# The first two blocks of a streaming encoder step: squares by quarters, early weight splitting, and one block's rstd taken from rows through DRAM

## The reference

```python
def rms_norm(x, g):
    x32 = x.astype(jnp.float32)
    y = x32 * lax.rsqrt(jnp.mean(x32 * x32, axis=-1, keepdims=True) + RMS_EPS)
    return (y * g.astype(jnp.float32)).astype(x.dtype)

def mixer_layer(x, hist_a, hist_b, norm_g, w_in, ...):
    hn = rms_norm(x, norm_g)
    proj = jnp.einsum('btd,de->bte', hn, w_in)          # 1024 -> 3584
    h_a, b_a, c_a, z_a, a_b, g_b, z_b = jnp.split(proj, SPLITS, axis=-1)
    conv_a, new_a = causal_dwconv(hist_a, c_a * h_a, conv_a_w)
    out_a = b_a * conv_a * jax.nn.silu(z_a)
    conv_b, new_b = causal_dwconv(hist_b, a_b * jax.nn.sigmoid(g_b), conv_b_w)
    s_b = jax.nn.silu(layer_norm(conv_b + conv_b_bias, ln_b_g, ln_b_b))
    out_b = s_b * jax.nn.silu(z_b)
    return x + jnp.concatenate([out_a, out_b], -1) @ w_out, new_a, new_b
```

## Time and profile before

| | |
|---|---|
| median of 3 runs | 1561.45 us (1558.83 to 1563.66) |
| the profiled execution | 1561.79 us, of which its span is 1560.0 us |
| TensorE busy | 1535.2 us, 98% of the span |
| VectorE, GpSimd, ScalarE busy | 81%, 37%, 34% |
| granted TensorE clock over the span | 0.999 |
| DMA, mean over the span | 230 GB/s, 358 MB |

### The profile page before, as it was taken

One profiled execution on the slowest core, in us unless ns is written; L12 is line 12 of the kernel. 1 busy time (PEld: TensorE's weight loads), 2 busy tenths in 40 slices (PEclk: granted clock), 3 DMA queues, 4 the chain that ended last, 5 costly groups with the idle time before them and its releaser, 6 DMA issues. The chain is left out here.

```text
span 1560.0 us, 19222 instructions
## 1 busy us (share of the span) xinstructions
PE 1535.2 (98%) x7228; PEld 1353.4 (87%) x7228; DVE 1265.7 (81%) x1179; ACT 538.1 (34%) x782; POOL 577.2 (37%) x494
## 2 busy tenths in 40 slices
PE   6999999999999999999999999999999999999998
PEld 6999999988888888888888888888897888888886
DVE  7699799998877998869798888789897577778753
ACT  5443433332242333332253312234524332332322
POOL 2766969112313121132221141146955233322310
PEclk9999999999999999999999999999999999999999
DMA  4987979788987789988779877757645433544432
GB/s 162 341 317 271 338 272 320 257 277 288 291 276 243 230 250 296 294 290 245 232 236 291 256 237 249 216 173 220 203 119 194 162 104 139 180 170 171 159 127 83
DMA packets 109648, 358.03 MB, mean 230 GB/s; under 512 B 16676, under 2 KB 20644, under 8 KB 105976
## 3 DMA queue, kind: packets, MB, share of 16 engines
q1 hardware_dynamic: 109560, 356.86, 69.6%
HBM read 263.02 MB, written 93.79 MB: 229 GB/s over the span
## 5 line engine op out<-in xcount | busy, mean ns | idle before, releaser
L1723 DVE SCALAR_TENSOR_TENSOR ps<-v,conv_b_taps,ps 128x920 f32<-128x920 f32 (+2 forms) x580 | 630.9, 1088 | 17.8
L1955 PE MATMUL ps<-xf,w_ring 128*128 128x460 f32 (+1 forms) x1624 | 603.0, 371 | 1.4 <-issue 0.9
L1957 PE MATMUL ps<-xf,w_ring 128*128 128x460 f32 (+1 forms) x1624 | 602.6, 371 | 0.0
L1956 PE MATMUL ps<-xf,w_ring 128*128 128x460 f32 (+1 forms) x1624 | 600.8, 370 | 0.0
L1955 PEld LDWEIGHTS ps<-xf,w_ring 128*128 128x128 f32 x1624 | 305.4, 188 | 36.1 <-issue 3.0
L1956 PEld LDWEIGHTS ps<-xf,w_ring 128*128 128x128 f32 x1624 | 305.4, 188 | 34.0
L1957 PEld LDWEIGHTS ps<-xf,w_ring 128*128 128x128 f32 x1624 | 304.9, 188 | 34.2
L1279 ACT ACTIVATE sets<-ps 128x460 f32<-128x460 f32 x168 | 92.8, 553 | 488.6 <-PE ps L1957 488.4
L1085 POOL TENSOR_TENSOR sets<-sets 128x460 f32<-128x460 f32 x42 | 56.1, 1335 | 415.4 <-ACT sets L1279 415.4
L1955 PE MATMUL ps<-w_out_split,mixed 128*128 128x512 f32 x512 | 199.9, 390 | 1.8 <-POOL mixed L1110 1.1
L1956 PE MATMUL ps<-w_out_split,mixed 128*128 128x512 f32 x512 | 199.5, 390 | 0.0
(11 more groups left out here) (173 smaller groups left out, 1665.1 us busy)
## 6 DMA issues: line engine op xcount, KB each, us to landing
w_ring<-weight_forms SPq DMA_DIRECT2D x294, 512.0 KB, 5.3
x_rows_again<-in_x_prompt SPq DMA_DIRECT2D x32, 512.0 KB, 4.3
out_y_prompt<-h_rows SPq DMA_DIRECT2D x32, 512.0 KB, 3.0
weight_forms<-xf SPq DMA_DIRECT2D x7, 2048.0 KB, 13.3
weight_forms<-w_ring SPq DMA_DIRECT2D x7, 2048.0 KB, 14.7
w_ring_f<-in_w_in SPq DMA_DIRECT2D x56, 256.0 KB, 3.2
xf_f<-in_w_in SPq DMA_DIRECT2D x26, 512.0 KB, 8.9
x_row<-in_x_prompt SPq DMA_DIRECT2D x28, 460.0 KB
```

Source lines behind the costliest of these rows:

```text
L1723: dve.scalar_tensor_tensor(dst, window, wb[:, j, k:k + 1], part, ALU.mult, ALU.add).then_inc(taps_done, 1)
L1955: pe.matmul(out, ahi, bhi, start=(start and x == 0), stop=False, skip_group_check=goes_on)
L1956: pe.matmul(out, ahi, blo, start=False, stop=False, skip_group_check=goes_on)
L1957: mm = pe.matmul(out, alo, bhi, start=False, stop=(stop and x == len(terms) - 1), skip_group_check=goes_on)
```

## The change

Four things are changed, all at the start of the program.

1. Block 0 comes in four quarters of 460 KB. ScalarE squares a quarter at a time, and VectorE adds each to a running sum as it comes.
2. The splitting of the first weights moves ahead: ScalarE does `weight_high(0, ...)` before the mean square of block 0, and VectorE does `weights_low(0)` as a whole before it scales x.
3. Block 1's mean squares no longer come from the channel-major copy. Its rows are loaded by four more transfers (`first_rows`, 115 partitions of 4096 bytes each, into ring space that the weights of period 1 use later), and ScalarE squares and sums each (`first_row_square`). These transfers stand between `load_w(0)` and `load_w(1)`; the channel-major block 1 now comes after `load_w(1)`.
4. Block 1's rstd is written to DRAM and read back into `spread`, behind the seven small loads on SP, and VectorE scales block 1 from there. `first_statistics(1)` and `first_rstd(1)` are gone from TensorE, and eight identity products are left of ten.

```diff
@@ -279,12 +279,10 @@
-        first_squares = [xf_f32[:, 6, :, :],
-                         ring_f32[:, 4:8, :, :].rearrange("p c l m -> p (c l m)")[:, 0:2 * HALF * TB]
-                         .rearrange("p (k t) -> p k t", t=TB)]
-
-        def first_stats(b):
-            return ps[0:STAT_ROWS, FIRST_BANK[b], 0:STAT_COLS]
+        first_squares = xf_f32[:, 6, :, :]
+        first_rows = ring_f32[0:STAT_ROWS, 4:8, :, :].rearrange("p c l m -> p c (l m)")
+        first_stats = ps[0:STAT_ROWS, FIRST_BANK, 0:STAT_COLS]
@@ -659,6 +661,8 @@
                 sp.wait_ge(rstd_out, 16 * stat_count(w, b))
+                if stat_count(w, b) == 1:
+                    sp.wait_ge(x01_scaled, 2 * KC)
                 need(sp, x_scaled, 8 * (stat_count(w, b) - 1))
@@ -818,17 +822,27 @@
+            for r in range(4):
+                src = A["xT"][0, :, r // 2].rearrange("p (k t) -> p k t", t=TB)
+                k = slice(2 * (r % 2), 2 * (r % 2) + 2)
+                sp.dma_start(st[:, r // 2, k, :], src[:, k]).then_inc(first_x_in[r], 16)
+            sp.dma_start(gain[:, :], A["norm_g"]).then_inc(gain_in, 16)
+            load_w(0)
+            for c in range(STAT_COLS):
+                sp.dma_start(first_rows[:, c, :], prompt_rows(1)[:, c, :]).then_inc(first_rows_in[c], 16)
+            load_w(1)
             for x in range(2):
-                src = A["xT"][0, :, x].rearrange("p (k t) -> p k t", t=TB)
-                sp.dma_start(st[:, x, :, :], src).then_inc(first_x_in[x], 16)
-            sp.dma_start(gain[:, :], A["norm_g"]).then_inc(gain_in, 16)
-            for x in range(2, 4):
-                src = A["xT"][1, :, x % 2].rearrange("p (k t) -> p k t", t=TB)
-                sp.dma_start(st[:, x, :, :], src).then_inc(first_x_in[x], 16)
-            load_w(0)
-            load_w(1)
+                src = A["xT"][1, :, x].rearrange("p (k t) -> p k t", t=TB)
+                sp.dma_start(st[:, 2 + x, :, :], src).then_inc(first_x_in[4 + x], 16)
             for dst, src in consts:
                 sp.dma_start(dst, src).then_inc(const_in, 16)
+            sp.wait_ge(x_rstd, 2)
+            at = P * STAT_COLS
+            dst = rstd_d[0, at:at + TB].rearrange("(r c) -> r c", c=STAT_COLS)
+            sp.dma_start(dst, x_rs[0:STAT_ROWS, STAT_COLS:2 * STAT_COLS]).then_inc(first_rstd_out, 16)
+            sp.wait_ge(first_rstd_out, 16)
+            sp.dma_start(spread[:, 0:TB], rstd_d[:, at:at + TB].to_broadcast([P, TB])).then_inc(first_rstd_in, 16)
             load_w(2)
@@ -963,6 +977,8 @@
                 pool.wait_ge(x_ms, count)
+                if count == 4:
+                    pool.wait_ge(first_rstd_out, 16)
                 need(pool, rstd_out, 16 * (count - 4))
@@ -1121,6 +1137,9 @@
             x_row_rstd(0, 1)
+            pool.wait_ge(first_row_sq, STAT_COLS)
+            pool.tensor_tensor(x_var[0:STAT_ROWS, STAT_COLS:2 * STAT_COLS], x_sq_sum[0:STAT_ROWS, STAT_COLS:2 * STAT_COLS],
+                               eps[0:STAT_ROWS, :].to_broadcast([STAT_ROWS, STAT_COLS]), ALU.add).then_inc(x_ms, 1)
             x_row_rstd(1, 2)
@@ -1188,15 +1207,20 @@
         def _(act):
-            def first_square(b, h):
-                act.wait_ge(first_x_in[2 * b + h], 16)
-                act.activation(first_squares[b][:, HALF * h:HALF * (h + 1), :], st[:, 2 * b + h, :, :], ACT.Square,
-                               scale=RMS_SCALE).then_inc(first_sq, 1)
-
-            def first_mean_square(b):
-                act.wait_ge(first_stat, b + 1)
-                act.activation(x_var[0:STAT_ROWS, STAT_COLS * b:STAT_COLS * (b + 1)], first_stats(b), ACT.Identity,
+            def first_square(r):
+                act.wait_ge(first_x_in[r], 16)
+                act.activation(first_squares[:, 2 * r:2 * r + 2, :], st[:, r // 2, 2 * (r % 2):2 * (r % 2) + 2, :],
+                               ACT.Square, scale=RMS_SCALE).then_inc(first_sq, 1)
+            def first_mean_square():
+                act.wait_ge(first_stat, 1)
+                act.activation(x_var[0:STAT_ROWS, 0:STAT_COLS], first_stats, ACT.Identity,
                                bias=eps[0:STAT_ROWS, :]).then_inc(x_ms, 1)
+            def first_row_square(c):
+                act.wait_ge(first_rows_in[c], 16)
+                act.activation(first_rows[:, c, :], first_rows[:, c, :], ACT.Square, scale=RMS_SCALE,
+                               accum_out=x_sq_sum[0:STAT_ROWS, STAT_COLS + c:STAT_COLS + c + 1]).then_inc(first_row_sq, 1)
@@ -1346,21 +1370,22 @@
-            first_square(0, 0)
-            first_square(0, 1)
-            first_square(1, 0)
-            first_square(1, 1)
-            act.wait_ge(ready0, 7)
-            first_mean_square(0)
+            for r in range(4):
+                first_square(r)
             weight_high(0, 0)
             weight_high(0, 1)
+            act.wait_ge(ready0, 7)
+            first_mean_square()
+            first_row_square(0)
+            first_row_square(1)
+            first_row_square(2)
             first_x_high(0, 0)
-            first_mean_square(1)
             first_x_high(0, 1)
+            first_row_square(3)
+            first_x_high(0, 2)
+            first_x_high(0, 3)
             weight_high(1, 0)
             weight_high(1, 1)
-            first_x_high(0, 2)
-            first_x_high(0, 3)
             evacuate(0, 0)
@@ -1516,28 +1541,32 @@
         def _(dve):
-            def first_sums(b):
-
-                sq = first_squares[b]
-                for h in range(2):
-                    dve.wait_ge(first_sq, 2 * b + h + 1)
-                    a = HALF * h
-                    dve.tensor_tensor(sq[:, a:a + 2], sq[:, a:a + 2], sq[:, a + 2:a + 4], ALU.add).then_inc(first_sum, 1)
-                dve.wait_ge(first_sum, 4 * b + 2)
-                dve.tensor_tensor(sq[:, 0:2], sq[:, 0:2], sq[:, HALF:HALF + 2], ALU.add).then_inc(first_sum, 1)
-                dve.wait_ge(first_sum, 4 * b + 3)
+            def first_sums():
+                sq = first_squares
+                for r in range(1, 4):
+                    dve.wait_ge(first_sq, r + 1)
+                    need(dve, first_sum, r - 1)
+                    dve.tensor_tensor(sq[:, 0:2], sq[:, 0:2], sq[:, 2 * r:2 * r + 2], ALU.add).then_inc(first_sum, 1)
+                dve.wait_ge(first_sum, 3)
                 dve.tensor_tensor(sq[:, 0:1], sq[:, 0:1], sq[:, 1:2], ALU.add).then_inc(first_sum, 1)
...
                 dve.wait_ge(gain_in, 16)
-                dve.wait_ge(first_spread, b + 1)
+                if b == 0:
+                    dve.wait_ge(first_spread, 1)
+                    rs = ps[:, FIRST_BANK, 0:TB]
+                else:
+                    dve.wait_ge(first_rstd_in, 16)
+                    rs = spread[:, 0:TB]
                 for k in ks:
-                    if k % HALF == 0:
-                        dve.wait_ge(first_x_in[2 * b + k // HALF], 16)
+                    if b == 0 and k % 2 == 0:
+                        dve.wait_ge(first_x_in[k // 2], 16)
+                    if b == 1 and k % HALF == 0:
+                        dve.wait_ge(first_x_in[4 + k // HALF], 16)
                     part = st[:, 2 * b + k // HALF, k % HALF, :]
-                    dve.scalar_tensor_tensor(part, part, gain[:, k:k + 1], ps[:, FIRST_BANK[b], 0:TB],
-                                             ALU.mult, ALU.mult).then_inc(x01_scaled, 1)
+                    dve.scalar_tensor_tensor(part, part, gain[:, k:k + 1], rs, ALU.mult, ALU.mult).then_inc(x01_scaled, 1)
@@ -1786,12 +1815,10 @@
-            first_sums(0)
-            first_sums(1)
+            first_sums()
+            weights_low(0)
             first_x_scale(0, range(HALF))
-            weights_low(0, [0])
             first_x_low(0, range(2))
-            weights_low(0, [1])
             first_x_scale(0, range(HALF, KC))
@@ -1958,21 +1985,20 @@
-            def first_statistics(b):
-
-                pe.wait_ge(first_sum, 4 * b + 4)
-                sq = first_squares[b][:, 0, :].rearrange("p (r c) -> p c r", c=STAT_COLS)
+            def first_statistics():
+                pe.wait_ge(first_sum, 4)
+                sq = first_squares[:, 0, :].rearrange("p (r c) -> p c r", c=STAT_COLS)
                 for c in range(STAT_COLS):
-                    mm = pe.matmul(first_stats(b)[:, c:c + 1], sq[:, c, :], ones[:, :], start=True, stop=True)
+                    mm = pe.matmul(first_stats[:, c:c + 1], sq[:, c, :], ones[:, :], start=True, stop=True)
                 mm.then_inc(first_stat, 1)
-            def first_rstd(b):
-
-                pe.wait_ge(x_rstd, b + 1)
-                to = ps[:, FIRST_BANK[b], 0:TB].rearrange("p (r c) -> p c r", c=STAT_COLS)
+            def first_rstd():
+                pe.wait_ge(x_rstd, 1)
+                to = ps[:, FIRST_BANK, 0:TB].rearrange("p (r c) -> p c r", c=STAT_COLS)
                 for c in range(STAT_COLS):
-                    col = STAT_COLS * b + c
```

(12 more changed lines are left out.)

10 lines of the change are left out of this document (7 added, 3 removed).

## The result

| | before | changed kernel |
|---|---|---|
| median of the runs | 1561.82 us (6 runs, 1558.83 to 1563.66) | 1572.09 us (6 runs, 1569.56 to 1573.41) |
| profiled execution | 1561.79 us, span 1560.0 | 1572.63 us, span 1570.8 |
| ratio | | 1.0066, 95% interval 1.0052 to 1.0080 |

The changed kernel is slower by 0.66%, about 10.3 us. The forecast was 1563.0, with a range from 1557.3 to 1567.5, and the measured time lies above it.

The account below looks back on a forecast made before the run. The prediction took TensorE, from the moment it is fed without a break, to bound the kernel. Its terms, +0.7 + 1.9 - 1.0 = +1.6 us, gave 1563.4, less 0.34 for the median: 1563.0, range 1557.3 to 1567.5.

Parts of the forecast that it names:

- Term 1: Block 0's quarters and early weight split: TensorE's statistics at 10.6 in place of 12.54, 1.9 us earlier; split costs nothing.
- Term 2: ScalarE's list: third row square, waiting for its row transfer, delays the first high part; first tile 0.7 us later, at 24.4.
- Term 3: TensorE's start: first matmuls run at the lower level for 5.4 us, +1.9 us (bounds -0.5 to +3.4).
- Term 4: TensorE's first tiles: `first_rstd(1)` no longer stands between two parts of tiles, -1.0 us.
- Term 5: Block 1's rstd through DRAM: scaling from 37.0, first low part at 43.0, 3.2 us before TensorE's need; no cost.
- Term 6: Later, GpSimd's sums: GpSimd falls 2.6 us back against TensorE, taken up by its 6.56 us wait; no cost.
- Rival C: GpSimd's lag in unit 0 shows after all: +2.6 us, 1565.6; chance 0.06.
- A: Row transfers at full rate, 1.12 us each, first tile at 20.0: -3.9 us, 1557.5; chance 0.14.
- B: Block 1's rstd trips through DRAM are slow, TensorE waits 6.8 us before tile (0,2): 1569.8; chance 0.13.

Follow-up runs that it names:

- e13: Kernel before, with GpSimd's first low sums not waiting for block 1's last low part and ScalarE making period 0's weight-sum high parts earlier; ratio 0.9995.
- e9: Changed kernel with the four row transfers issued behind the second weights and block 1's x; one run, 1572.84 us.
- e1: Changed kernel with each row transfer issued as two, partitions 0 to 111 and 112 to 114; ratio 0.9997 to the kernel before.
- e2: Kernel before with block 0 squared by quarters and the first weights split ahead of rstd, no row transfers; ratio 1.0010.
- e3: Changed kernel with ScalarE's four row squares moved behind the high parts of block 0 and of the second weights; ratio 1.0077 to the kernel before.
- e11: e10 with the trip of block 1's rstd through DRAM ahead of SyncE's seven small loads; ratio 1.0003 to the kernel before.
- e7: Kernel before with five idle operations on GpSimd ahead of its first low sums; ratio 1.0040, 6.2 us slower.
- e10: Changed kernel with each row transfer over 128 partitions instead of 115; ratio 0.9999 to the kernel before.
- e16: Changed kernel with block 1's rstd spread by TensorE into PSUM in place of the trip through DRAM; ratio 1.0054 to the kernel before.
- e15: e10 with block 1's rstd spread by TensorE into PSUM in place of the trip through DRAM; ratio 0.9985 to the kernel before.
- e17: e16 with 33 identity products in place of 8 before the first tile; ratio 1.0041 to the kernel before.

## Why the prediction was wrong

**The premise failed.** "What is gained or lost before the first tile moves the end of the kernel one for one, as long as no later chain runs dry" was drawn from TensorE's waits. A later chain was already level with it, within 0.4 us by e13. The profile had it: VectorE at 119.5 of 124 us after 56 us. TensorE's 98% hid it, because VectorE came just in time.

**Term 1, quarters: right.** Statistics at 11.07 (forecast 10.6), scaling from 16.57 (16.3). The early split cost nothing.

**Term 2, rows: right in kind, far too small.** The place was named (third row square ahead of the first high part), and 3.6 us for a row transfer alone is what e9 and the last gap show. But the rows share the queues with weights and x, and then all sixteen engines fall to 244 GB/s; the share was 1.04 from 14 to 24 us where the forecast looked for 0.31. Rows came 6.3 and 5.4 apart, the first tile at 29.87 in place of 24.4. The term was +6.2, not +0.7, which is 5.5 of the 9.1 us between forecast and median.

**Term 3, TensorE's rate: right.** 14 matmuls took 5.23 us (29.87 to 35.10), where 14 at 0.204 are 2.86: 2.4, less the 0.5 of before, +1.9 as forecast. It rested on the assumption that the lower level lasts about as it did before. In e1, e2 and e3, where TensorE waited 0.3 to 0.7 us ahead of the first tile in place of 10.9, no matmul was slow there.

**Term 4: right,** -1.0. TensorE reached tile (0,2) at 51.78, 7.1 after the earlier trace rows; 6.2 + 1.9 - 1.0 is that.

**Term 5: no wait at tile (0,2), right, but not by its numbers.** SyncE was through with the small loads at 37.9 instead of 32.2: in the timeline the issue of one small load lasts 7.18 us while the rows move, where with rows over 128 partitions (e11) none lasts over 1.2. The two trips took 5.6 (37.98 to 43.60), forecast 4.8. TensorE was late enough to be served.

**Term 6 failed as the premise did.** The lag was put at 2.6 and said to be taken up by GpSimd's wait. It was 3.6 (10.7 - 7.1), and it showed; these are the rest of the 9.1. e7 alone, 5.2 of such lag at a cost of 6.2, refutes the reasoning. The 6.56 us of slack were GpSimd's; VectorE, which it feeds, was idle for 4.5 us in the 124 after 56. Rival C had said that the lag shows, at 2.6, but by a wait of TensorE on weights, and the trace has waits on VectorE's sets, sums and x. A and B did not happen.

Taken apart by runs: with the rows at full rate (e10) all of the 10.3 us is gone (-0.2 is left), with rstd back in PSUM alone (e16) 1.9 of it, by intervals that overlap, with both (e15) 12.6. The rows are the loss. Where they are out of the way, the SBUF source of the scaling costs 3.1 us on VectorE (8.04 against 4.91) and about 2 of the whole, again by intervals that overlap (e10 and e15).

## What to carry to other kernels

Before one wait of the fullest engine is made the measure, look at the other engines in the same stretch: one that is 96% busy from some point on carried most of a delay of its first operation to the end here (e7), whatever slack its supplier shows. A transfer that doesn't span 128 partitions is priced with its company, not by itself. An operand that moves from PSUM to SBUF can put VectorE in GpSimd's way, and a wait between the two may be there to keep them apart.

## What the runs showed of the hardware

- VectorE and GpSimd slow each other when VectorE's operation reads two SBUF tiles: eight scalings 12.09 or 8.04 us beside GpSimd, 4.95 with it idle; four low parts 9.01 against 4.19; GpSimd 2.18 against 1.31. With one source in PSUM nothing is lost (4.91). The Trainium skill, SBUF - State Buffer, section "Who interferes with whom", says so: a VectorE instruction with two SBUF inputs contends with a GpSimd instruction that reads SBUF. The traces agree.
- Partitions of each row transfer and the rate of all traffic beside it, at a share of 1.03 or 1.04: 128, 413 GB/s; 112 + 3, 274; 112 + 16, 253; 64 + 64, 229; 115, 244; 115 with nothing beside it, 130 to 132 at share 0.34.
- TensorE's granted clock in the changed kernel was 1.00 (2.4 GHz) while the products ran, 16.3 to 19.0, and 0.50 (1.2 GHz) from 22 on, when it had been idle since 19.0; its first 14 matmuls, at 0.50, came 0.37 us apart in place of 0.20. In e17 they did so after an idle time of 5.07 us.
